# Two padded convolution inputs, TensorE-weighted parts of a step, and a level fill of taps in the differential-attention stage of a two-block transformer kernel

## The reference

```python
h = rms_norm(x, attn_norm_w[l]); proj = h @ w_in[l]
q, k, v, u, g = jnp.split(proj, splits, axis=-1)
q = rms_norm(q.reshape(B, S, N_HEADS, 2, HEAD_DIM), q_norm_w[l])      # k likewise
p = probs(qb1, k1f) - lamf * probs(qb2, k2f)      # two causal softmax maps, with a relative bias
a = einsum('bhqk,bhkd->bhqd', p, vf); a = rms_norm(a, subln_w[l]) * (1.0 - lam_init)
u_a, u_b = jnp.split(u, 2, axis=-1)
c = causal_depthwise_conv(u_a * jax.nn.sigmoid(u_b), conv_w[l], conv_b[l])      # 31 taps
```

## Time and profile before

| | |
|---|---|
| median of 3 runs | 3442.72 us (3442.67 to 3446.35) |
| the profiled execution | 3441.59 us, its span 3439.5 us |
| TensorE products | 2974.0 us busy, 86% of the span |
| VectorE | 1580.6 us, 46% |
| ScalarE, GpSimd | 1234.6 us (36%), 710.0 us (21%) |
| the stage's 64 steps | from 1318 to 2213 us of the span |

### The profile page before, as it was taken

How to read it: one execution, slowest core, us unless ns; L and a number is a source line. 1 busy time by engine, 2 the same in 40 slices (tenths; PEclk the granted TensorE clock), 3 DMA queues, 4 the chain that set the end, 5 groups by cost and what they waited for, 6 DMA issues and landing times. The chain is left out here.

```text
span 3439.5 us, 35301 instructions
## 1 busy us (share of the span) xinstructions
PE 2974.0 (86%) x13448; PEld 2400.5 (70%) x13448; DVE 1580.6 (46%) x1931; ACT 1234.6 (36%) x2003; POOL 710.0 (21%) x317
## 2 busy tenths in 40 slices
PE   6999998777778769889898999694985999998998
PEld 5787886656667557667677678582775877787786
DVE  3666652356763237787777766514222220111121
ACT  3555542334531235455544555423113110111110
POOL 2111121100012112332233323212211212121111
PEclk8999999988999879999999999897998999999999
DMA  4112122132233112121211222241420111111112
GB/s 109 43 44 62 56 74 64 21 62 44 51 110 135 55 65 63 44 62 51 63 39 56 63 63 74 104 129 55 146 93 18 49 37 49 43 49 43 43 43 74
DMA packets 239268, 218.87 MB, mean 64 GB/s; under 512 B 29304, under 2 KB 200856, under 8 KB 239128
## 3 DMA queue, kind: packets, MB, share of 16 engines
q1 hardware_dynamic: 238096, 215.41, 20.6%
q10 hardware_dynamic: 1032, 1.57, 0.3%
HBM read 156.66 MB, written 41.42 MB: 58 GB/s over the span
## 5 line engine op out<-in xcount | busy, mean ns | idle before, releaser
L179 POOL TENSOR_TENSOR w_lo<-w_raw,w_hi 128x1024 fp32r<-128x1024 f32 (+3 forms) x228 | 535.2, 2349 | 2124.8 <-ACT w_hi L171 2124.8
L171 ACT ACTIVATE w_hi<-w_raw 128x1024 fp32r<-128x1024 f32 (+3 forms) x228 | 224.1, 986 | 787.6 <-PE u_y_ps L1763 222.3
L2386 DVE SCALAR_TENSOR_TENSOR d_acc<-d_padded,vectors,d_acc 128x1024 f32<-128x1024 f32 x240 | 397.3, 1655 | 4.5
L197 PE MATMUL d_pp<-h_hi,w_hi 128*128 128x512 f32 x896 | 367.7, 410 | 12.3 <-PEq L67 5.2
L197 PE MATMUL d_pp<-h_hi,w_lo 128*128 128x512 f32 x896 | 368.3, 411 | 0.0
L197 PE MATMUL d_pp<-h_lo,w_hi 128*128 128x512 f32 x896 | 365.3, 408 | 0.0
L197 PE MATMUL s_pp<-h_hi,w_hi 128*128 128x512 f32 x512 | 206.8, 404 | 11.9 <-PEq L67 11.9
L197 PEld LDWEIGHTS d_pp<-h_hi,w_hi 128*128 128x128 f32 x896 | 174.6, 195 | 56.3 <-issue 18.0
L2170 POOL TENSOR_TENSOR d_probs<-d_probs 128x128 f32<-128x128 f32 (+3 forms) x64 | 123.5, 1929 | 410.7 <-ACT d_probs L2284 410.6
L197 PE MATMUL s_pp<-h_hi,w_lo 128*128 128x512 f32 x512 | 205.4, 401 | 0.0
L197 PE MATMUL s_pp<-h_lo,w_hi 128*128 128x512 f32 x512 | 204.6, 400 | 0.0
(11 more groups left out here) (333 smaller groups left out, 6511.3 us busy)
## 6 DMA issues: line engine op xcount, KB each, us to landing
w_raw<-in_w_in SPq DMA_DIRECT2D x97, 512.0 KB, 4.0
w_raw<-in_w_gate_up SPq DMA_DIRECT2D x44, 512.0 KB, 3.9
w_raw<-in_w_down SPq DMA_DIRECT2D x22, 512.0 KB, 3.7
gates<-s_gate SPq DMA_DIRECT2D x16, 512.0 KB, 5.2
f_gate<-gates SPq DMA_DIRECT2D x16, 512.0 KB, 5.2
w_raw<-in_w_out SPq DMA_DIRECT2D x16, 512.0 KB, 3.8
w_raw<-in_w_proj SPq DMA_DIRECT2D x16, 512.0 KB, 4.7
x_tok_in<-in_x SPq DMA_DIRECT2D x8, 512.0 KB, 7.4
```

Of the source, the lines that this page charges most:

```text
L171: act.activation(self.hi[:, s, 0:chunks, :], self.raw[:, s, 0:chunks, :], ACT.Copy).then_inc(self.rounded[s], 1)
L179: pool.tensor_tensor(self.lo[:, s, 0:chunks, :], self.raw[:, s, 0:chunks, :], f32(self.hi[:, s, 0:chunks, :]), ALU.subtract).then_inc(self ...
L197: mm = pe.matmul(halves(ps)[h], w[:, k, :], x[:, k, h * HALF:(h + 1) * HALF], start=(k == 0 and r == 0), stop=(k == chunks - 1 and r == 2))
L2386: dve.scalar_tensor_tensor(out=acc[:, :], in0=x, scalar=wt, in1=acc[:, :], op0=ALU.mult, op1=ALU.add).then_inc(c["taps"], 1)
```

## The change

`d_padded` gets a second buffer, so that heads alternate; `feed_conv` of head h now waits for the taps of head h - 2, and taps of a head may stand up to part 16 (step 5, part 1) of the head in which the next "a" comes; those of the next head begin in part 17. `d_raw` loses the buffer of v: v goes into k's buffer (v of head 0 into `d_o_sb`), with waits that keep k and v apart. The tiles' products are shared out by `pe_work`, so that each part has about equal TensorE time with the rest of what stands in it. `values` and the first `turn_t`, `round_t` and `low_t` move from part 0 to part 1, the second ones keep part 2. The taps are shared out by filling each part's VectorE load to one level (`dve_work`). `store_conv` comes later in SyncE's list. k's square follows the emptying of the tiles in its part.

```diff
-        raw = mem.sb("d_raw", [P, 3, TOK])
+        raw = mem.sb("d_raw", [P, 2, TOK])
-        padded = mem.sb("d_padded", [P, PAD + TOK])
+        padded = mem.sb("d_padded", [P, 2, PAD + TOK])
+        v_raw = [o_sb] + [raw[:, 1, :]] * LAST
-        weight = [13, 13, 13, 13, 12, 12, 11, 11]
+        V_TURN, Q_SQUARE, O_SQUARE, K_SQUARE = 4, 5, 6, 8
+        def pe_work(h, at):
+            b, x = divmod(at, PARTS)
+            turned = min(4, b) if b else 4
+            work = {V_TURN: 0.9, Q_SQUARE: 1.7 * (h < LAST), O_SQUARE + 1: 1.7 * (h > 0),
+                    K_SQUARE + 1: 1.7 * (h < LAST)}.get(at, 0)
+            if x == 0:
+                work += 0.23 * (b + 1)
+            if x == 1:
+                work += 0.11 * turned + {1: 2.9, 3: 0.7, 5: 1.5, 7: 2.2}.get(b, 0)
+            if x == 2:
+                work += 0.11 * (max(b - 4, 0) if b else 4)
+            return work
...
-            total = each[h] * SIX
-            at = [base + total * sum(weight[:b]) // sum(weight) for b in range(QB + 1)]
+            fixed = [pe_work(h, at) for at in range(PARTS * QB)]
+            room = 0.231 * each[h] * SIX
...
+            total, share = 0.0, [max(level - f, 0) for f in fixed]
...
-        conv_end = [part_of[stream.index(("a", h)), 0] - 2 for h in range(1, HEADS)] + [PARTS * (STEPS - 1)]
+        conv_end = [at + 1 for at in conv_in_at[1:]] + [PARTS * (STEPS - 1) + 1]
...
-            room = range(conv_in_at[h] + 1, conv_end[h] + 1)
+            room = range(conv_in_at[h] + (2 if h else 1), conv_end[h] + 1)
...
+            level = (sum(dve_work(at) for at in room) + TAP * n) / len(room)
+            free = [max(level - dve_work(at), 0.2) for at in room]
...
-            conv_after = {tile_at(conv_end[h]): h for h in range(LAST)}
+            conv_after = {tile_at(conv_end[h] + 1): h for h in range(LAST)}
...
                         if what == "k":
                             act.wait_ge(c["k_low"], 2 * n)
+                            act.wait_ge(c["v_turned"], 2 * n)
                         if what == "v":
-                            act.wait_ge(c["v_turned"], 2 * n)
+                            act.wait_ge(c["k_low"], 2 * n + 2)
...
-                    if x in (0, 2) and 0 <= u < STEPS and x // 2 < CHUNKS[u % QB]:
-                        round_t(u, x // 2)
+                    if x > 0 and 0 <= u < STEPS and x - 1 < CHUNKS[u % QB]:
+                        round_t(u, x - 1)
                     if x == 0 and s < STEPS:
                         weigh(s)
...
-                    if h:
-                        dve.wait_ge(c["taps"], CONV * h)
+                    if h >= 2:
+                        dve.wait_ge(c["taps"], CONV * (h - 1))
...
-                    if x == 0 and s >= 3 and s % 2 == 1:
+                    if x == 1 and s >= 3 and s % 2 == 1:
                         values((s - 3) // 2)
...
-                    if x in (0, 2) and 0 <= u < STEPS and x // 2 < CHUNKS[u % QB]:
-                        turn_t(u, x // 2)
+                    if x > 0 and 0 <= u < STEPS and x - 1 < CHUNKS[u % QB]:
+                        turn_t(u, x - 1)
```

More of the change, by code:

```diff
@@ L2021, in differential_and_conv @@
         TILES = len(stream)
-        weight = [13, 13, 13, 13, 12, 12, 11, 11]
+        V_TURN, Q_SQUARE, O_SQUARE, K_SQUARE = 4, 5, 6, 8
[11 more added lines that the diff above has]
+            return work
         ends, base = [], 0
         for h in range(HEADS):
-            total = each[h] * SIX
-            at = [base + total * sum(weight[:b]) // sum(weight) for b in range(QB + 1)]
-            base += total
-            ends += [[lo + (hi - lo) * x // PARTS for x in range(PARTS + 1)] for lo, hi in zip(at, at[1:])]
+            fixed = [pe_work(h, at) for at in range(PARTS * QB)]
+            room = 0.231 * each[h] * SIX
+            level = 0.0
+            for lower in sorted(fixed):
+                under = [f for f in fixed if f <= lower]
+                if sum(lower - f for f in under) <= room:
+                    level = (room + sum(under)) / len(under)
+            total, share = 0.0, [max(level - f, 0) for f in fixed]
+            at = [base]
+            for x in share:
+                total += x
+                at.append(base + round(each[h] * SIX * total / sum(share)))
+            base += each[h] * SIX
+            ends += [at[PARTS * b:PARTS * (b + 1) + 1] for b in range(QB)]
         def part(s, x):
@@ L2072, in differential_and_conv @@
+            if x == 2 and (b == 0 or b > 4):
+                load += 0.15 + 0.135 * (b - 4 if b else 4)
+            return load
         taps_in = {}
         for h in range(HEADS):
-            room = range(conv_in_at[h] + 1, conv_end[h] + 1)
+            room = range(conv_in_at[h] + (2 if h else 1), conv_end[h] + 1)
             n = CONV - (TAPS_FIRST if h == 0 else 0)
-            time, other = [sum(f(at) for at in room) for f in (pe_load, dve_load)]
-            share = (other + TAP * n) / time
@@ L2078, in differential_and_conv @@
-            done, t, o = 0, 0.0, 0.0
-            for at in room:
-                t, o = t + pe_load(at), o + dve_load(at)
-                upto = n if at == room[-1] else min(n, max(done, int((share * t - o) / TAP)))
+            level = (sum(dve_work(at) for at in room) + TAP * n) / len(room)
+            free = [max(level - dve_work(at), 0.2) for at in room]
+            total, done = 0.0, 0
+            for at, x in zip(room, free):
+                total += x
+                upto = n if at == room[-1] else round(n * total / sum(free))
@@ L2387, in tap, with taps @@
                                              op1=ALU.add).then_inc(c["taps"], 1)
[L2389 removed]
+            def taps(at, first_half):
                 if at in taps_in:
                     h, x, y = taps_in[at]
[L2393 removed]
+                    middle = x + (y - x + (at % PARTS == 0)) // 2
+                    for t in range(x, middle) if first_half else range(middle, y):
                         tap(h, t)
```

48 lines of the change are left out of this document (23 added, 25 removed).

## The result

The change makes the kernel slower: 3497.64 us median (3489.21 to 3500.21, 4 runs) against 3444.45 us of the kernel before beside it, ratio 1.0151, 95% interval 1.0136 to 1.0165. The profiled execution took 3495.57 us, its span is 3493.5 (before 3439.5). The forecast of 3473 has the direction and the range of 3425 to 3507 holds the time, but the loss is 53 us where 31 were forecast.

What follows compares the result with a forecast made beforehand. It took VectorE's in-order round trips with ScalarE as the bound: 87.2 + 24.4 + 11.9 - 4.8 = 118.7 us for a middle head. Over all heads, +30.5 on 3441.6 gave 3472.1, and 1.1 for the median 3473 us; range 3425 to 3507.

Steps and rivals of the forecast that it cites:

- 24.4 + 11.9: In a head like head 2, VectorE's waits of 24.4 us before the change, plus 11.9 us more waiting.
- the exponentials' waits: VectorE's waits ahead of `weights`: 7.7 us before, +1 as steps 7 and 3 lose taps and steps 0 to 2 gain one.
- those of the norms and high parts: VectorE's waits for norms and q's high part, behind scalings and a square: 9.9 us before, about 10.9 after, +1.
- Sigmoid and `round_t`: Before `low_t`: sigmoid of b behind step 4's exponentials, +5.5 us; `round_t` behind the scalings in other steps, +1.3 us.
- Store: Between a head's last tap (part 16) and the next head's tap 0 (part 17), VectorE waits for the store: +3.6 us.
- Work absorbed and avoided, 4.8: Of 12.4 us a head by which GpSimd slows taps, 3 us absorbed in waits and 1.8 us avoided.
- Head 0 ... 107.5, -1: First head: 5 taps fewer than before, no step 4 sigmoid, no output norm: 118.7 - 3.6 - 5.5 - 2.1 = 107.5 us, -1.
- Head 6 ... about 115: Head 6, with 28 taps against 26: about 115 us against 111.2, +4.
- Head 7 ... TensorE is its bound: 0: Last head: no norms of q and k, TensorE its bound, so no change, 0 us.
- Levelling (1): Rival: VectorE keeps up, TensorE is the bound, heads 1 to 4 lose their TensorE waits: 3376 us, or 3409; chance 0.17.
- Contention (2): Rival: spread taps contend less with GpSimd, 9 of 12.4 us a head go: about no change, 3441 us; chance 0.12.
- Much slower (4): Rival: TensorE at half speed after new waits makes VectorE wait too, 5 us a head more, above 3507 us; chance 0.08.

Runs made afterwards that it cites:

- The first edit: Changed kernel with 3 products moved from step 4's first part to step 3's last in heads 1 to 4, so the sigmoid precedes step 4's exponentials: 3489.64 us.
- the third: Changed kernel with ScalarE's scalings of a step moved from part 0 to part 1, behind `round_t`: 3475.53 us, ratio 1.0095.
- the kernel with the taps alone: Kernel before plus second padded input, v in k's buffer, level fill of taps and later store, its own parts kept: 3485.55 us, ratio 1.0125.
- the fourth mend: Changed kernel with sigmoid, store and scalings mended, plus one product of b's second half moved to step 3's part 2 in heads 5 and 6: 3428.57 us, ratio 0.9962.
- the taps of before: Changed kernel with the tap table, one-buffer waits and store place of the kernel before: 3479.82 us, ratio 1.0096.
- three mends: Changed kernel with 3 products moved ahead of step 4, next head's taps one part later, and scalings behind `round_t`: 3440.0 us, ratio 0.9986.
- the taps of before and two mends: Changed kernel with the old tap table, waits and store place, b's second half before step 4, and scalings behind `round_t`: 3455.81 us, ratio 1.0043.
- the short `mix`: `mix` adds only the first 128 columns of the two maps: on the changed kernel 3489.9 us, on the kernel before 3422.6 us.

## Why the forecast was right, and where its size was off

- **The mechanism.** Right for the middle heads. VectorE's waits of head 2 were forecast at 24.4 + 11.9 = 36.3 us and are 36.7; its work at 87.2 - 4.8 = 82.4 and is 83.0 (119.7 less the waits). Heads 1 to 5 came out 4 us longer in all than the sum said. That is no luck of one total: the exponentials' waits were forecast at 8.7 us and are 9.0, those of the norms and high parts at 10.9 and are 10.6.
- **Sigmoid and `round_t`.** Forecast waits before `low_t` in the steps 0, 1, 4, 5, 6, 7: 0.5, 1.9, 5.5, 0.9, 2.8, 1.5; measured 0.54, 1.50, 5.54, 0.87, 2.76, 1.55. The first edit, which takes the sigmoid out of this round trip, and the third, which puts the scalings behind `round_t` again, show the causes; but the terms are not what undoing them gives back. The sigmoid's +5.5 gives 2.5 us a head, and the late scalings, priced at +1.3, give 3.4, since they also shorten waits of step 4, of the norms and of q's high part.
- **Store.** Forecast 3.6, measured 4.3: the transfer lands in 4.1 us in the median, not the 3.0 of the earlier trace rows. In the kernel with the taps alone it lands in 2.7 and the wait is 2.8.
- **Work absorbed and avoided, 4.8.** Measured 4.2. The group of taps, before and after:

```profile
L2386 DVE SCALAR_TENSOR_TENSOR d_acc<-d_padded,vectors,d_acc 128x1024 f32<-128x1024 f32 x240 | 397.3, 1655 | 4.5
L2414 DVE SCALAR_TENSOR_TENSOR d_acc<-d_padded,vectors,d_acc 128x1024 f32<-128x1024 f32 x240 | 376.2, 1568 | 3.4
```

  1568 ns in the mean, 1655 before (over all 240; the 228 of the earlier trace rows have 1666): 31 x 0.087 is 2.7 us a head. In head 2 itself the taps take 46.9 us where they took 49.8, 2.9 less; the rest is in other instructions of VectorE.
- **"Head 0 ... 107.5, -1".** Mis-sized, the largest term: it took 114.9, 7.4 more. The sum took 11.2 us off head 2 for what head 0 lacks. Two of its three subtractions, read in the order of its list (taps, sigmoid, norm), failed. The 3.6 for three taps fewer: its 28 taps take 46.5 us, the 31 of head 2 take 46.9, so 0.4. The 5.5 for the sigmoid: head 0 has none in step 4, but no tap either, and VectorE waits there for the scalings and `round_t` alone:

```profile
1379.88 0.69 DVE L2501 TENSOR_TENSOR d_t_lo<-d_bank,d_t_hi 128x512 fp32r<-128x512 f32 x1 [2.10 <-ACT d_t_hi L2318]
```

  So 3.4 and not 5.5. Beside that it has one wait of 2.3 us for TensorE's scores that the sum had not. Its waits are 35 us where the sum makes about 30.
- **"Head 6 ... about 115".** Mis-sized by 6.7: 121.9. The sum shows no working for this head; +4 with two taps more leaves some 1.4 us for more waiting. Its waits went from 32.4 to 40.5 us, those for `low_t` as follows (before, after):

```profile
DVE d_t_lo L2472 <- ACT d_t_hi L2292: 12.9, 8, 4.9
...
DVE d_t_lo L2501 <- ACT d_t_hi L2318: 19.2, 9, 4.3
```

  The longest of each is the sigmoid's, in step 3, in both kernels; the fourth mend takes it away, but it is no part of the loss. The loss lies in steps 4 to 7: 2.10, 2.90 + 1.27, 2.52 and 2.74 us, 11.5 in all, where they had 3.0. These are the round trips of the middle heads again. Had the sum put the middle heads' +11.9 - 4.8 and two taps on top of 111.2, it would have come to 121.
- **"Head 7 ... TensorE is its bound: 0".** Mis-sized: head 7 and all behind it take 1337.2 us where they took 1330.4, +6.8. The waits of TensorE and VectorE there, from 2156 us on:

```profile
PE d_bank L341 <- DVE d_t_lo L2501: 11.8, 6, 4.5
...
DVE d_t_lo L2501 <- ACT d_t_hi L2318: 23.2, 12, 3.2
```

  TensorE waits for `low_t`, 11.8 us where it was 3.7, and `low_t` for `round_t`. With the scalings behind `round_t` the stretch takes 1333.9, with the taps of before 1331.3, so the first alone takes back about half of it and the second most of it. That TensorE bounds this head was put down without a row; `low_t` sets it too.
- These and 4.0 of heads 1 to 5 make 7.4 + 6.7 + 6.8 + 4.0 - 1.3 (an earlier start of the stage) = 23.6, the gap from 30.5 to the spans' 54.0.
- **Rivals.** Levelling (1) asked for VectorE's waits under 24.4 a head; they are 36.7. With three mends they are 19.4, heads 1 to 4 are 2.2 to 4.8 us shorter than before, and the kernel is as fast as before or a trace faster (0.9986); with the taps of before and two mends they are 22.9 and the kernel is slower (1.0043). So waits under 24.4 alone don't decide, and the 67 us of this rival never came. By the rule of the Trainium skill that it cited (Perfetto Trace Analysis, Identifying the Most-Contended Engine) the busiest engine would be the one to relieve. The traces agree that VectorE sets the pace; but its busy time fell by 28 us, its share from 75% to 67% (639 of 950 us), and the kernel became slower. Contention (2) came about in part and was outweighed. Much slower (4) did not: VectorE never waits for TensorE in head 2.

## What to carry to other kernels

Where two engines hand work back and forth in fixed orders, sum the waits of the engine that sets the pace and ask of every moved instruction which round trip it fills or lengthens; busy shares and levelled loads don't tell that. Do the sum for each kind of period (first, last, the one with more tiles) with its own order of instructions: the middle heads came out to 1%, and 21 of the 24 us missed lay in the first head and the last two, which were priced by a subtraction, by a round number and at nothing. A wait that is mended may be worth all of itself or nothing, depending on what the engine runs into next, so try mends together before a change is given up: alone they gave 8, 17 and 22 us, together 58. And before a mended kernel is held against the old one, ask whether the old one has the mended fault too, as it had the fourth.

## What the runs showed of the hardware

A tap and an instruction of GpSimd that reads SBUF take turns. In the rows of step 5 above the first tap starts 0.06 us ahead of the subtraction and takes its full-speed 1.28 us, while the subtraction takes 3.43 instead of the 2.38 it takes in step 4, where VectorE stands almost from its start on:

```profile
1613.58 2.38 POOL L179 TENSOR_TENSOR w_lo<-w_raw,w_hi 128x1024 fp32r<-128x1024 f32 x1 [15.11 <-ACT w_hi L171]
```

The tap that starts within the subtraction ends only 1.1 us behind it, whether it started 0.7 us before its end (at 1632.41) or 1.7 us (at 1627.21). `low_t`, which reads one of its inputs from PSUM, takes 0.68 beside the same subtraction. So in these rows the one that starts first runs on, and the order of starts decides who pays; GpSimd, with much idle time, can pay, VectorE can't. This is what the Trainium skill (SBUF — State Buffer, Who interferes with whom) states as an exclusive lock for an instruction of VectorE with two SBUF inputs, and by its rule of one SBUF input `low_t` should be free of it; the trace agrees with both. For the 95 instructions of a head VectorE's busy time lay between 79.8 and 89.4 us over these kernels, by order alone and the short `mix`.
